# A two-block transformer with routed experts: routing split in two, a layer's norms placed between the combines, the output stored by token tiles

## The chip, the cores and the metric

The kernel runs on one core of a Trainium2 chip. All five engines of the core run their own instruction streams and meet only at semaphores: TensorE (PE, matmuls), VectorE (DVE), ScalarE (ACT), GpSimd (POOL) and SyncE (SP), which here only issues the loads of weights, the fetch of expert rows and the like. The metric is the device time of one execution in microseconds, lower is better.

## The reference

Everything is float32. Two blocks of two layers each run one after the other, on 256 tokens of width 1024. The first block (two attention mixers, each with a squared-ReLU MLP) is not touched by the change. The second block has an image stream `x` (256 tokens) and a context stream `ctx` (256 tokens); each of its two layers is a mixer and a mixture of experts. Layer 0 routes both streams (512 tokens), layer 1, the last, only `x` (256 tokens). Cut to what matters here:

```
def _moe(h, grp_w, grp_b, exp_w, exp_b, w_gate, w_up, w_down):
    g_logits = h @ grp_w + grp_b                      # 4 groups
    g_sel = argmax(g_logits);  g_w = softmax(g_logits)[g_sel]
    e_logits = (h @ exp_w + exp_b)[group g_sel]       # 8 experts of that group
    e_p, e_i = top_k(softmax(e_logits), 2)
    wts = g_w * e_p / sum(e_p)
    # each token goes to two of the 32 experts; each expert computes
    #   (silu(x @ w_gate[e]) * (x @ w_up[e])) @ w_down[e]
    # and a token's result is the weighted sum of its two rows
for i in range(2):
    hx, hc = modulate(rmsnorm(x)), modulate(rmsnorm(ctx))
    yx, yc = mixer(hx, hc);  x = x + g1 * yx          # ctx too in layer 0
    x = x + g2 * _moe(modulate(rmsnorm(x)), ...)      # ctx too in layer 0
```

An expert has 6 MB of weights, and each layer streams those of all 32 experts.

## The kernel before, in words

**Weights.** A ring of six slots of 2 MB holds weight tiles. SP issues one load for each tile, in one fixed order over the whole kernel (L1629 in its helper `load`), and waits before each until the tile that had the slot has been used. In a mixture-of-experts stage (`moe_loads`) an expert takes three tiles: gate, up, down. SP runs ahead of PE until the ring is full, so up to six tiles are there when the first expert begins.

**Routing.** `pe_moe` computes the logits of T token tiles of 128 (T is 4 in layer 0, 2 in layer 1; L985), and turns the tokens back to rows (L993), which ACT copies and stores to `tokens_d` (L1115, L1118). `dve_moe` then walks through one chain of small VectorE instructions, in which `do(...)` makes each wait for the one before: the best group of each token (L1204 to L1208), the two best experts in it (L1212 to L1218), one-hot marks `hot` of both picks (L1221), their sum `picked` (L1223) and its prefix over token tiles `prefix` (L1225). PE multiplies these by a strictly lower triangle and by ones (L999, L1000), which gives every token its rank within its expert. An expert's block has 64 slots; tokens beyond go to up to 15 overflow blocks. So DVE finds which experts have extra blocks and a running sum over experts (L1234 to L1244), each pick's position, block number and slot (L1248 to L1263), and makes two one-hot matrices, `slot_hot` and `blk_hot` (32 blocks and 15 overflow blocks, 47 columns; L1264 to L1270). PE multiplies them into a table of token ids for each block and slot (L1006). From it DVE computes `idx`, the rows to gather (L1282 to L1287), and `row`, where results go (L1291).

**Experts.** POOL gathers the 64 tokens of a block by an indirect DMA (L1363), two blocks ahead; PE turns them (L1017); DVE copies them out (L1309); PE runs gate and up (`inner`: L1026, L1029), turns the hidden rows (L1035) and runs down (`outer`: L1044), one expert behind; ACT applies silu (L1133) and copies the results out (L1136); POOL scatters them to `rows_d` (L1369). The hardware loop covers experts 1 to 30, with the last one and the overflow block behind it. Each engine reads the number of overflow blocks from memory into a register (`value_load`): before the experts on PE, ACT, DVE and POOL, behind the loads on SP (L1708 ff). With these inputs layer 0 has one overflow block and layer 1 has none.

**Combine.** When all rows are stored, SP fetches them by token tile (L1412); ACT weights the first row of each pair (L1178), and DVE adds the second, applies the gate and adds to the residual, three instructions for each tile (L1340, L1342, L1343), in layer 0 in the order ctx 0, ctx 1, x 0, x 1.

**The next layer's norms.** DVE makes the rotary tables (`rope_tables`, L2010, L2015) from three small loads that POOL issues once the rows are stored (L2152, L2154). `act_norm` squares and sums each token tile and takes the root (L350, L344), DVE divides (L365, L367), PE turns (L338), ACT and DVE evict four parts each (L387, L391). The ctx norm `L1.nc` runs whole and then the x norm `L1.nx`; then PE starts the projection (L438).

**End.** POOL stores both output tiles in one DMA of 1 MB (L2187) after the last combine.

## Time and profile before

| | |
|---|---|
| median of three runs | 2433.67 us (2433.35 to 2438.34) |
| the profiled execution, its own time | 2432.66 us |
| its span in the profile | 2430.8 us |
| PE / DVE / ACT / POOL busy, share of the span | 86% / 32% / 15% / 8% |
| granted TensorE clock, mean | 0.935 |
| layer 0's experts | about 1184 to 1715 us |
| layer 1's experts | about 1912 to 2402 us |
| weights of 65 expert blocks | 195 loads of 2048 KB |

Times in the profile are microseconds from the start of the span. 1.9 us of the execution's own time lie outside the span. The shares are means over stages with different limits: the page's row of forty slices shows the DMA engines at 9 tenths all through both expert stages, and close to idle just ahead of each. A clock of 1.00 is 2.4 GHz and 0.50 is 1.2 GHz.

### The profile page before, as it was taken

To read this page: it belongs to the slowest core of one execution; us is meant where nothing else is said; L and a number is where in the kernel's file an instruction comes from. 1 tells how busy PE (TensorE), PEld (TensorE's weight loads), DVE (VectorE), ACT (ScalarE), POOL (GpSimd) and SP (SyncE) were. 2 spreads that over 40 slices of the span, in tenths; PEclk is the share of its full clock that TensorE was granted. 3 is DMA by queue.
4 is the path that set the end of the run, shared out by engine and by line. 5 is a ranking of instruction groups with operands and counts; after the bars stand their busy time and mean duration, and the time that the engine had idled before them with its cause. 6 is when DMAs were issued, how large, how long until landed. Compare 5 with 4: busy or idle time off the path is not lost. (4 is left out here: it accounts for less than half of the span.)

```text
span 2430.8 us, 22184 instructions
## 1 busy us (share of the span) xinstructions
PE 2089.8 (86%) x8645; PEld 1111.1 (46%) x8645; DVE 768.4 (32%) x1684; ACT 360.5 (15%) x775; POOL 185.0 (8%) x225
## 2 busy tenths in 40 slices
PE   6998999998999998877698888888387798888884
PEld 3456666444666576435344343333254343333331
DVE  1225773214777118932311111101442310111111
ACT  2232000123100122421100000000232100000000
POOL 0000000000000000000011011111000011111110
PEclk9999999999999999998799899899799799999997
DMA  9931788341687503002499999999732499999994
GB/s 255 300 134 70 285 299 302 124 157 67 231 292 287 206 19 139 1 18 90 153 407 407 404 412 405 401 413 380 269 128 90 162 416 422 417 414 419 403 416 176
DMA packets 128053, 631.53 MB, mean 260 GB/s; under 512 B 14262, under 2 KB 16470, under 8 KB 102128
## 3 DMA queue, kind: packets, MB, share of 16 engines
q1 hardware_dynamic: 109056, 592.94, 62.0%
q0 software_dynamic: 17744, 34.33, 5.2%
q10 hardware_dynamic: 1184, 3.35, 0.4%
q8 instruction: 42, 0.69, 0.1%
q14 instruction: 27, 0.22, 0.0%
HBM read 625.47 MB, written 26.57 MB: 268 GB/s over the span
## 5 line engine op out<-in xcount | busy, mean ns | idle before, releaser
L1026 PE MATMUL PS<-ring,arena 128*64 128x512 f32 x1040 | 519.0, 657 | 112.5 <-DMA ring<-ex_up 110.6
L1029 PE MATMUL PS<-ring,arena 128*64 128x512 f32 x1040 | 519.8, 658 | 0.0
L1026 PEld LDWEIGHTS PS<-ring,arena 128*64 128x64 f32 x1040 | 151.1, 151 | 393.2 <-issue 382.6
L438 PE MATMUL PS<-ring,arena 128*128 128x512 f32 (+1 forms) x736 | 297.4, 560 | 7.6 <-issue 5.2
L1309 DVE COPY arena<-PS 128x512 f32<-128x512 f32 x64 | 44.3, 692 | 673.3 <-PE PS L1017 673.3
L1044 PE MATMUL PS<-ring,arena 128*64 128x512 f32 x1040 | 237.5, 598 | 1.6 <-DVE arena L1305 1.6
L757 PE MATMUL PS<-arena,ring 128*128 128x256 f32 x1024 | 226.6, 383 | 2.9 <-DVE arena L389 1.5
L768 PE MATMUL PS<-ring,arena 128*128 128x512 f32 x512 | 222.2, 592 | 0.0
L757 PEld LDWEIGHTS PS<-arena,ring 128*128 128x128 f32 x1024 | 194.8, 191 | 40.0 <-issue 13.7
L438 PEld LDWEIGHTS PS<-ring,arena 128*128 128x128 f32 x736 | 138.1, 191 | 147.5 <-issue 138.9
L1029 PEld LDWEIGHTS PS<-ring,arena 128*64 128x64 f32 x1040 | 151.0, 151 | 4.3
L768 PEld LDWEIGHTS PS<-ring,arena 128*128 128x128 f32 x512 | 97.2, 190 | 116.0 <-issue 115.3
L1133 ACT ACTIVATE arena<-PS 64x512 f32<-64x512 f32 x65 | 38.3, 590 | 663.3 <-PE PS L1026 652.1
L716 PE MATMUL PS<-ring,arena 128*128 128x512 f32 x288 | 126.7, 601 | 10.4 <-issue 9.6
L1044 PEld LDWEIGHTS PS<-ring,arena 128*64 128x64 f32 x1040 | 69.5, 136 | 118.1 <-issue 112.0
L1363 POOL DMA_INDIRECT arena<-tokens_d,arena x65 | 61.6, 947 | 697.0 <-PE PS L1017 619.6
L852 DVE SCALAR_TENSOR_TENSOR modacc<-ring,silu_c,modacc 128x512 f32<-128x512 f32 x168 | 112.8, 748 | 0.0
L852 DVE SCALAR_TENSOR_TENSOR xn<-ring,silu_c,xn 128x512 f32<-128x512 f32 x168 | 112.8, 747 | 0.0
L1017 PEld LDWEIGHTS PS<-const,arena 64*128 64x128 f32 x585 | 84.9, 245 | 60.8 <-issue 51.1
L338 PE MATMUL PS<-const,xn 128*128 128x128 f32 x176 | 35.6, 387 | 83.1 <-DVE xn L367 83.1
L1017 PE MATMUL PS<-const,arena 64*128 64x64 f32 x585 | 94.0, 304 | 9.4 <-DMA arena<-tokens_d,arena 9.4
L716 PEld LDWEIGHTS PS<-ring,arena 128*128 128x128 f32 x288 | 55.2, 193 | 80.3 <-issue 79.0
(229 smaller groups left out, 1653.6 us busy)
## 6 DMA issues: line engine op xcount, KB each, us to landing
ring<-ex_gate SPq DMA_DIRECT2D x65, 2048.0 KB, 16.8
ring<-ex_up SPq DMA_DIRECT2D x65, 2048.0 KB, 14.7
ring<-ex_down SPq DMA_DIRECT2D x65, 2048.0 KB, 24.0
ring<-ffn_w SPq DMA_DIRECT2D x32, 2048.0 KB, 12.8
ring<-mod_w SPq DMA_DIRECT2D x24, 2048.0 KB, 8.1
ring<-a_w_qkv SPq DMA_DIRECT2D x9, 2048.0 KB, 35.7
ring<-b_w_qkv SPq DMA_DIRECT2D x6, 2048.0 KB, 12.9
ring<-w_in_ab SPq DMA_DIRECT2D x3, 2048.0 KB
```

Source lines behind the costliest of these rows:

```text
L438: mm = pe.matmul(PS[:, u % 4, 0:w.width], q.src[:, k, w.t * P:(w.t + 1) * P], w8(w.tile, w.width)[:, k, :], start=(k == 0), stop=(k == KD ...
L716: mm = pe.matmul(PS[:, u % 8, :], x.src(k)[:, w.t * P:(w.t + 1) * P], rhs, start=(i == 0), stop=(i == len(w.terms) - 1))
L757: mm = pe.matmul(PS[:, b, (c % 2) * 2 * P:(c % 2 + 1) * 2 * P], w8(tile)[:, k, c * P:(c + 1) * P], XL[:, k, :], start=(k == 0), stop=(k == ...
L768: mm = pe.matmul(PS[:, 4 + 2 * t + h, :], hiddenT[:, half, c, t * P:(t + 1) * P], w4(tile)[:, c, h * BANK:(h + 1) * BANK], start=first and ...
L852: ins = dve.scalar_tensor_tensor(acc, w, silu_c[:, k, v:v + 1], acc, ALU.mult, ALU.add)
L1017: mm = pe.matmul(PS[:, 4 + u, k * CAP:(k + 1) * CAP], Xg[0:CAP, u, :].rearrange("p (m k) -> p k m", k=KD)[:, k, :], ident[0:CAP, 0:CAP], s ...
L1026: g = pe.matmul(PS[0:CAP, u, :], xT[:, k, :], w8(gate)[:, k, :], start=(k == 0), stop=(k == KD - 1))
L1029: h = pe.matmul(PS[CAP:P, u, :], xT[:, k, :], w8(up)[:, k, :], start=(k == 0), stop=(k == KD - 1))
L1044: mm = pe.matmul(PS[h * CAP:(h + 1) * CAP, 2 + u, :], hidT[:, k, :], w4(tile)[:, k, h * BANK:(h + 1) * BANK], start=(k == 0), stop=(k == 3))
L1133: act.activation(swish[CAP:P, :], PS[0:CAP, u, :], ACT.Silu).then_inc(done, 1)
L1309: dve.tensor_copy(XgT[:, u, :], PS[:, 4 + u, :]).then_inc(s.xT, 1)
L1363: pool.indirect_dma_start(out=Xg[0:CAP, u, :], out_offset=None, in_=tokens_d, in_offset=bass.IndirectOffsetOnAxis(ap=m.idx[0:CAP, blk:blk ...
```

## The change

- **Constants.** Token codes become `PLACES - code` (PLACES is 2048), so that an empty slot, a zero, maps by one multiply-add to an index past the end; `first` and `full` are new.
- **Routing, first part.** The group is found by a reduction, a comparison, a product and a reduction over all tiles at once. `prefix` is gone; PE makes the ranks from `picked` by one triangle product and T products with ones. `slot_hot` is made directly from the rank, and a first table of token ids has only the 32 experts' first blocks. One instruction gives `idx`, one gives `row`, and POOL starts to gather.
- **Routing, second part.** `place_overflow` (running sum, block, slot, marks of the overflow blocks, the number of extra blocks) stands on DVE behind `tokens_out(0, 0)`; its table of ids is a second pair of products on PE behind the hardware loop, and there the engines now read the number of blocks. The weights of the two picks come after the first hidden rows.
- **Token stores** of tiles 2 and 3 use their own buffer.
- **Norms.** In layer 0's combine DVE makes the rotary tables ahead of the first tile (`first`); the ctx norm's rows are made after the third tile (`after`). The x norm gets its own PSUM banks, columns and a scratch area; ACT sums x 0 ahead of evicting the ctx norm, and PE doesn't wait between the two norms.
- **Output.** SP stores each token tile, 512 KB, as soon as it is combined.

```
@@ pe_moe
-            pe.matmul(PS[:, 5, 0:(T + 1) * NE], ones, m.prefix..., start=True, stop=False)
-            mm = pe.matmul(PS[:, 5, 0:T * NE], C("before"), m.picked..., start=False, stop=True)
+            pe.matmul(PS[:, 5, 0:(T + 1) * NE], C("before"), m.picked..., start=True, stop=False)
+            for t in range(T):
+                mm = pe.matmul(PS[:, 5, (t + 1) * NE:(T + 1) * NE]..., ones,
+                               m.picked[:, t:t + 1, :].to_broadcast([P, T - t, NE]), start=False, stop=(t == T - 1))
-            pe.wait_ge(s.placed, b0.placed + 2)
...
-            pe.wait_ge(s.routed, b0.routed + 2)
+            def slot_ids(marks, first, width):
+                for half in range(2):
+                    for n in range(2 * T):
+                        mm = pe.matmul(PS[half * CAP:(half + 1) * CAP, 7, first:first + width], m.slot_hot[:, n, :],
+                                       marks[:, n, :], start=(n == 0), stop=(n == 2 * T - 1))
+                    mm.then_inc(s.ids, 1)
+            pe.wait_ge(s.placed, b0.placed + 1)
+            slot_ids(m.hot_token.rearrange("p j t e -> p (j t) e"), 0, NE)
             at(pe, (s.token_copied, T))
-            extra = pe.value_load(...)
...                                          # behind the loop over the experts
                 hidden_turned(e + 1)
+            pe.wait_ge(s.placed, b0.placed + 2)
+            slot_ids(m.over_hot, NE, OVER)
+            pe.wait_ge(s.routed, b0.routed + 2)
+            extra = pe.value_load(...)
             inner(NE - 1, 1, W.tail[0:2])
@@ dve_moe
-            do(dve.tensor_copy(m.g8[:, :, 0:EG], m.logits[:, :, 0:EG]))
-            for t in range(T):
-                do(dve.max(m.gtop[:, t, :], m.g8[:, t, :]))
-                do(dve.max_index(m.gidx[:, t, :], m.gtop[:, t, :], m.g8[:, t, :]))
-            do(dve.tensor_copy(m.gsel, m.gidx[:, :, 0]))
+            do(dve.tensor_reduce(m.gtop, groups, AX, ALU.max))
+            do(dve.tensor_tensor(m.gmark, groups, over(m.gtop, shape, 2), ALU.is_equal))
+            do(dve.tensor_tensor(m.gmark, m.gmark, over(C("first"), shape, 1), ALU.mult))
+            do(dve.tensor_reduce(m.gsel, m.gmark, AX, ALU.max))
...
-            do(dve.tensor_tensor(m.picked, m.hot[:, 0], m.hot[:, 1], ALU.add))
-            for t in range(T):
-                ins = dve.tensor_tensor(m.prefix[:, t + 1, :], m.prefix[:, t, :], m.picked[:, t, :], ALU.add)
+            dve.tensor_tensor(m.picked[:, 0:T, :], m.hot[:, 0], m.hot[:, 1], ALU.add).then_inc(s.picked, 1)
...
+            for j in range(2):
+                do(dve.tensor_tensor(m.hot_token[:, j], m.hot[:, j], over(code[j], shape, 2), ALU.mult))
             dve.wait_ge(s.rank, b0.rank + 1)
+            for j in range(2):
+                do(dve.tensor_tensor(m.tmp[:, j], m.hot[:, j], rank, ALU.mult))
+            do(dve.tensor_reduce(pos, tmp, AX, ALU.add))
+            dve.tensor_tensor(m.slot_hot, over(C("slot"), [P, n, CAP], 1), over(pos, [P, n, CAP], 2),
+                              ALU.is_equal).then_inc(s.placed, 1)
...
+            def rows_of(first, last, idx_done, row_done):
+                dve.wait_ge(s.ids, b0.ids + 1 + 2 * (first > 0))
+                idx_done(dve.tensor_scalar(m.idx[0:CAP, first:last], PS[0:CAP, 7, first:last], -0.25, PLACES / 4,
+                                           ALU.mult, ALU.add))
+                dve.wait_ge(s.ids, b0.ids + 2 + 2 * (first > 0))
+                row_done(dve.tensor_scalar(m.row[:, first:last], PS[:, 7, first:last], -2.0, C("half"),
+                                           ALU.mult, ALU.add))
...
             tokens_out(0, 0)
+            place_overflow()
             tokens_out(1, 1)
             hidden_out(0, 0, m.T.head[1])
+            weights()
...                                          # behind the loop
+            rows_of(NE, NB, ...)
+            dve.wait_ge(s.routed, b0.routed + 2)
+            extra = dve.value_load(...)
             hidden_out(NE - 1, 1, m.T.tail[1])
...
+            if first:
+                first()
             dve.wait_ge(second[m.l].s.gate2, ...)
             for n, t in enumerate(combine_order(T)):
...
+                if after:
+                    after(n)
@@ pool_moe
-            pool.wait_ge(s.routed, b0.routed + 2)
-            extra = pool.value_load(...)
+            pool.wait_ge(s.routed, b0.routed + 1)
...
                 if e == NE:
+                    pool.wait_ge(s.routed, b0.routed + 3)
+                    extra = pool.value_load(...)
@@ the streams of ACT, DVE, SP and POOL
-            act_norm(act, L1.nc)
-            at(act, L1.nc.turned)
-            act_norm(act, L1.nx)
+            act_norm_sums(act, L1.nc)
+            act.wait_ge(moes[0].s.combined, moes[0].b.combined + 3)
+            act_norm_sum(act, L1.nx, 0)
+            norm_out(act, L1.nc, 0)
+            act_norm_sums(act, L1.nx, tiles=(1,))
+            norm_out(act, L1.nx, 0)
...
-            dve_moe(dve, moes[0])
-            rope_tables(L1)
-            dve_norm(dve, L1.nc)
-            dve_norm(dve, L1.nx)
+            def norms_beside(n):
+                if n == 2:
+                    dve_norm_rows(dve, L1.nc)
+            dve_moe(dve, moes[0], first=lambda: rope_tables(L1), after=norms_beside)
+            at(dve, L1.nc.turned)
+            dve_norm_rows(dve, L1.nx)
+            norm_out(dve, L1.nc, 1)
+            norm_out(dve, L1.nx, 1)
...
+            for n, t in enumerate(combine_order(2)):
+                sp.wait_ge(moes[1].s.combined, moes[1].b.combined + n + 1)
+                sp.dma_start(out[0][t * P:(t + 1) * P, :], hx[:, t, :]).then_inc(s_out, 16)
...
-            pool.dma_start(out[0].rearrange("(t p) d -> p t d", p=P), hx[:, :, :]).then_inc(s_out, 16)
```

## Rows read from the trace of the kernel before

**Rows 1.** Windows: PE, PEld, DVE, ACT, POOL busy; clock; DMA share; GB/s.
```profile
1300.00:1680.00 380.00, 327.88 (x1450) 147.85 (x1448) 42.09 (x70) 27.63 (x47) 44.75 (x46) 0.92 1.01 408
1184.00:1194.00 10.00, 9.86 (x34) 3.04 (x35) 0.09 (x1) 0.20 (x1) 0.93 (x1) 0.74 0.03 7
```

**Rows 2.** Timeline of SP: start, duration, engine, line, what it issued.
```profile
1123.10 0.33 SPq L1629 DMA_DIRECT2D ring<-ex_gate  x1
1193.80 0.33 SPq L1629 DMA_DIRECT2D ring<-ex_up  x1
```

**Rows 3.** Timeline of layer 0's routing; in brackets the idle time before and its releaser.
```profile
1155.55 0.31 DVE L1202 TENSOR_TENSOR arena<-PS,arena 128x144 f32<-128x144 f32 x1 [12.36 <-issue]
...
1158.29 0.28 DVE L1212 TENSOR_TENSOR arena<-const,arena 128x128 f32<-128x128 f32 x1
...
1159.92 1.09 PE L993 MATMUL PS<-const,arena 128*128 128x128 f32 x8 [0.23 <-ACT xn L1115]
...
1162.32 0.87 DVE L1225 TENSOR_TENSOR arena<-arena 128x32 f32<-128x32 f32 x4
...
1163.24 0.54 PE L999 MATMUL PS<-arena,ones 128*128 128x160 f32 x2 [2.23 <-DVE arena L1225]
...
1164.04 0.29 DVE L1231 COPY arena<-PS 128x128 f32<-128x128 f32 x1 [0.85 <-PE PS L1000]
...
1174.34 3.25 PE L1006 MATMUL PS<-arena 128*64 128x47 f32 x32 [10.34 <-DVE arena L1270]
...
1176.78 0.18 DVE L1287 TENSOR_SCALAR arena<-arena 64x47 uint32<-64x47 f32 x1
...
1178.72 1.01 POOL L1363 DMA_INDIRECT arena<-tokens_d,arena  x1 [48.31 <-issue]
```

**Rows 4.** Group by line and shape on DVE: busy us, mean ns of one.
```profile
L1264 DVE TENSOR_TENSOR arena<-const,arena 128x512 f32<-128x512 f32 x1 | 0.7, 691 | 0.0
```

**Rows 5.** Timeline of layer 1's routing, half the token tiles.
```profile
1895.17 0.46 PE L999 MATMUL PS<-arena,ones 128*128 128x96 f32 x2 [2.01 <-DVE arena L1225]
...
1906.95 0.99 POOL L1363 DMA_INDIRECT arena<-tokens_d,arena  x1 [28.51 <-issue]
```

**Rows 6.** Timeline of layer 0's combine and of the norms behind it.
```profile
1719.42 0.56 POOL L2154 DMA_DIRECT2D arena<-k_norm_c  x1
...
1724.16 1.28 DVE L1340 SCALAR_TENSOR_TENSOR arena<-arena 128x1024 f32<-128x1024 f32 x1 [14.49 <-ACT arena L1178]
...
1734.02 1.04 ACT L350 ACTIVATE xn<-arena 128x1024 f32<-128x1024 f32 x1
...
1737.84 0.29 ACT L344 ACTIVATE small<-small,const 128x1 f32<-128x1 f32 x1
...
1740.47 0.28 DVE L2010 TENSOR_TENSOR arena<-arena 128x128 f32<-128x128 f32 x1
...
1741.41 0.16 DVE L365 RECIPROCAL small<-small 128x1 f32<-128x1 f32 x1
...
1754.74 14.00 PE L438 MATMUL PS<-ring,arena 128*128 128x512 f32 x32 [1.77 <-DVE arena L391]
```

**Rows 7.** DMA issues: KB each, median us from issue to landing.
```profile
arena<-k_norm_c POOLq DMA_DIRECT2D x1, 32.0 KB, 8.8
```

**Rows 8.** Timeline at the end of the experts: SP's loads, PE's waits.
```profile
1671.61 0.33 SPq L1629 DMA_DIRECT2D ring<-ex_down  x1
1673.61 0.35 SPq L1712 DMA_DIRECT2D ring<-ex_gate  x1
...
1697.95 1.12 PE L1026 MATMUL PS<-ring,arena 128*64 128x512 f32 x1 [3.11 <-DMA ring<-ex_up]
...
2385.51 0.61 PE L1026 MATMUL PS<-ring,arena 128*64 128x512 f32 x1 [0.47 <-DMA ring<-ex_up]
```

**Rows 9.** DMA issues: KB each, median us from issue to landing.
```profile
out<-hx POOLq DMA_DIRECT2D x1, 1024.0 KB, 4.5
...
tokens_d<-xn ACTq DMA_DIRECT2D x4, 512.0 KB, 2.7
```

More of the change, by code:

```diff
@@ L87, in shape_constants @@
     parts["slot"] = np.tile(np.arange(CAP), (P, 1))
-    parts["block"] = np.tile(np.arange(NB), (P, 1))
+    parts["block"] = np.tile(np.arange(OVER), (P, 1))
     parts["expert"] = np.tile(np.arange(NE), (P, 1))
-    parts["group"] = np.tile(np.arange(NE) // EPG, (P, 1))
+    parts["group"] = np.tile(EG - np.arange(NE) // EPG, (P, 1))
+    parts["first"] = np.tile(EG - np.arange(EG), (P, 1))
+    parts["full"] = np.tile(CAP * np.arange(1, FULL + 1), (P, 1))
     parts["over"] = np.tile(np.repeat(np.arange(OVER), NE), (P, 1))
     token = p[:, None, None] + P * np.arange(4)[None, None, :]
-    parts["token"] = 4 * token + np.arange(2)[None, :, None] + 1
-    parts["half"] = p[:, None] // CAP
+    parts["token"] = PLACES - (4 * token + np.arange(2)[None, :, None])
+    parts["half"] = 2 * PLACES + p[:, None] // CAP
     parts["eps"] = np.full((P, 1), EPS)
@@ L1179, in act_moe, with dve_moe @@
                    .then_inc(s.weighted, 1)
-        def dve_moe(dve, m):
+        def dve_moe(dve, m, first=None, after=None):
             s, b0, T, n = m.s, m.b, m.tiles, 2 * m.tiles
@@ L1243, in dve_moe @@
-            through = x
-            do(dve.tensor_tensor(m.before, through, m.extra, ALU.subtract))
-            tmp = m.tmp.rearrange("p j t e -> p (j t) e")
-            for j in range(2):
-                do(dve.tensor_tensor(m.tmp[:, j], m.hot[:, j], m.rank, ALU.mult))
-            do(dve.tensor_reduce(flat(m.pos), tmp, AX, ALU.add))
-            do(dve.tensor_tensor(tmp, hot, over(m.before, [P, n, NE], 1), ALU.mult))
-            do(dve.tensor_reduce(flat(m.start), tmp, AX, ALU.add))
-            pos, start, turn, spill = flat(m.pos), flat(m.start), flat(m.turn_no), flat(m.spill)
@@ L1262, in dve_moe @@
-            do(dve.tensor_tensor(blk, blk, esel, ALU.add))
-            do(dve.scalar_tensor_tensor(slot, turn, -float(CAP), pos, ALU.mult, ALU.add))
-            dve.tensor_tensor(m.slot_hot, over(C("slot"), [P, n, CAP], 1), over(slot, [P, n, CAP], 2),
-                              ALU.is_equal).then_inc(s.placed, 1)
-            do(dve.tensor_tensor(m.blk_hot, over(C("block"), [P, n, NB], 1), over(blk, [P, n, NB], 2),
-                                 ALU.is_equal))
-            for j in range(2):
-                part = m.blk_hot[:, j * T:(j + 1) * T, :]
-                ins = dve.tensor_tensor(part, part, over(C("token")[:, 4 * j:4 * j + T], [P, T, NB], 2), ALU.mult)
-                if j:
-                    ins.then_inc(s.placed, 1)
@@ L1298, in dve_moe @@
-            dve.sem_inc(s.weights_ready, 1)
-            extra = dve.value_load(m.regs[0:1, OVER:OVER + 1], min_val=0, max_val=m.over)
+            dve.tensor_tensor(m.picked[:, 0:T, :], m.hot[:, 0], m.hot[:, 1], ALU.add).then_inc(s.picked, 1)
+            dve.tensor_scalar(m.ngtop, m.gtop, -1.0, None, ALU.mult).then_inc(s.group_top, 1)
+            dve.tensor_tensor(m.gap, m.etop[:, :, 1], m.etop[:, :, 0], ALU.subtract).then_inc(s.expert_gap, 1)
+            code = [C("token")[:, 4 * j:4 * j + T] for j in range(2)]
@@ L1592, in moe_stage @@
             m.pos, m.start, m.turn_no = take(2, tiles), take(2, tiles), take(2, tiles)
-            m.spill, m.blk, m.slot = take(2, tiles), take(2, tiles), take(2, tiles)
-            m.slot_hot, m.blk_hot = take(n, CAP), take(n, NB)
+            m.blk, m.slot = take(2, tiles), take(2, tiles)
+            m.slot_hot, m.over_hot = take(n, CAP), take(n, OVER)
             m.idx, m.row = take(NB, dt=U32), take(NB, dt=U32)
-            m.empty, m.code = take(NB), take(NB)
             m.full_before = take(OVER, NE)
```

180 lines of the change are left out of this document (92 added, 88 removed).

## The prediction

> **What bounds the kernel now.** I read the page's forty slices first: the DMA engines are at 9 tenths through both expert stages and nearly idle in the slices ahead of each. The windows say the same with a number: over 380 us of layer 0's experts the DMA share is 1.01 and 408 GB/s flow [rows 1]. PE is the busiest engine by share, but there it waits for tiles. So the expert stages last as long as their weights take to stream, and what can be gained is the time in which the stream stands. SP's timeline shows that time. A load is issued at 1123.10 and the next at 1193.80 [rows 2]: the ring is full, and its first slot comes free only when PE has done gate and up of expert 0. That needs the gather, which needs the routing. Layer 1 repeats the pattern. Every microsecond by which a first gather comes earlier starts the stream earlier, and as the amount of data is the same, it ends earlier by as much. The same holds for the norms between the layers, where PE waits from the end of the experts until 1754.74 [rows 6], and for the last store, which nothing follows.
>
> The chain of layer 0's routing is in the timeline [rows 3]: logits at 1155.55, first ranks product at 1163.24, ranks read at 1164.04, ids product at 1174.34, idx done at 1176.78 + 0.18 = 1176.96, gather at 1178.72. All but PE's share is small DVE instructions: one of 0.18 us costs 0.21 with its gap to the next.
>
> **Routing, layer 0.** From the end of the logits' step (1155.89) to L1212 (1158.29) 2.40 us are spent on the group. Four small steps replace it, 0.82: 1.6 saved. One cast in place of two and the gap moved away: 0.3. The prefix, 0.87, goes. `picked` would be ready at 1162.32 - 1.9 = 1160.45. But PE is still turning the last token tile until 1159.92 + 1.09 = 1161.0, and the ranks wait behind it. The new ranks product is five float32 products, ten pieces, where there were two in four pieces, 1163.24 to 1164.04, 0.20 each. Narrower pieces gain nothing visible, so I price by the piece: 1.9 to 2.0 us. Ranks are there at 1163.0, 1.0 us earlier than before. (Bounds: priced by columns, 480 against 288, it is 1.35; by pieces 2.0.) The two multiplies by the code lie under it.
>
> Then come two multiplies at 0.33 (as the copy of ranks, 0.29, with its gap), a reduction of 256 columns between those and the 0.69 of 512 columns [rows 4], say 0.45, and `slot_hot`, 0.69 plus the signal: 1.85. PE starts the ids at 1164.9, not 1174.34. From there to idx took 2.62 before, with three DVE steps; one remains, so 2.2. The count of full blocks (three steps, 1.0 us) lies under PE's half of the ids. idx is done at 1167.1, 9.9 us earlier. POOL then no longer loads a register ahead of the gather. SP's timeline prices that: from 1671.94 to 1673.61 it does two loads and a branch [rows 8], so about 0.8 for one. Layer 0 gains 10.7. (Bounds: 9.4 with a free-standing rank penalty of 0.5 more and no gain at POOL, 11.5 with ranks by columns and no wait left but 0.8.) The token stores land 2.7 us after issue [rows 9], before that time.
>
> **Routing, layer 1.** Half the tiles. The group's part shrinks from 2.40 to about 1.43 and the new one is again 0.82: 0.6. Casts 0.3, prefix 0.43. The ranks start at 1895.17 - 1.35 = 1893.8 [rows 5], PE being free; three products, 1.2. The four DVE steps at half width, between 0.18 and layer 0's values, 1.35; eight pieces of ids (3.25 / 32 = 0.10 each) with latency 0.9; idx 0.2; POOL 0.8. The gather starts at 1898.25, not 1906.95 [rows 5]: 8.7. (Bounds 7.5 to 9.5.)
>
> **The second part** stands behind `tokens_out(0, 0)`. DVE's queue behind it is `tokens_out(1, 1)` and the hidden rows of expert 0, and PE waits for those only after gate and up of expert 0, which fill the window 1184 to 1194 [rows 1]. Twelve scan steps, about fifteen small ones, a `slot_hot` at 0.69 and two row-0 steps near 0.6 make 7.2 us against 9.5 of cover. Cost nothing; without cover it would be up to 7.2.
>
> **Behind the loop** PE gets 32 pieces of ids in layer 0 (3.25) and 16 in layer 1 (1.6), and a register load, 0.75. In layer 0 the overflow block absorbs part: PE waited 3.11 us there for its weights [rows 8], 2.4 of it usable after ACT's copy, and a little before expert 31. 4.0 - 2.8 leaves 1.2. In layer 1 PE runs from 2385.51 through to the end of the experts with only 0.47 of waiting ahead [rows 8], so 2.35 - 0.5 = 1.9 is on the path. POOL's scatter of expert 28 now waits for the second ids; expert 30's copy, a gate and up and a down product later, is the first to need it. Bounds: 0 and 6.3 together. I take 3.1.
>
> A rule of the Trainium skill bears on the register load: "Runtime: NRT & Kernel Launch", section "Instruction fetch mechanics", gives about 0.2 us for a bulk register load from HBM. By that the two insertions would cost 1.1 less and the two gathers gain 1.1 less; the sum would stay.
>
> **Norms.** Before, four combines follow each other, then tables, then the ctx norm, then the x norm. The new order hides the ctx norm beside the last combine, and PE needn't wait between norms. But `first` puts the tables ahead of the combines, and they need three POOL loads. The last is issued at 1719.42 and takes 8.8 us to land [rows 6, 7]: 1728.2. The tables take 0.94 (1740.47 to 1741.41), so the first combine starts at 1729.2, not 1724.16. Behind it on DVE is everything. Combines of 3.75 us (three of up to 1.28) end at 1732.95, 1736.7 and 1740.4. ACT's sums of ctx take from 1734.02 to 1738.13 before, 4.1; they now start at 1736.75 and end at 1740.85. DVE makes the ctx rows until 1742.4 and the last combine until 1746.2. ACT's sum for x 1 ends 1.5 later, 1747.8; its row is ready at 1748.8; DVE then evicts four parts of ctx and four of x, 1.95 each, until 1752.7. PE starts at 1752.75 where it was 1754.74 [rows 6]: 2.0 gained. With the tables free it would be 5.5. The weights of this projection are there by then either way.
>
> **Store.** The last tile's 512 KB go from SP. The token stores of that size landed in 2.7 us, the whole output took 4.5 [rows 9]: 1.8. The first tile's store lies under the second combine. What follows the landing I take as unchanged.
>
> Against splitting speaks the Trainium skill, "DMA: Bandwidth & Descriptors", section "Anatomy of one DMA": about 2 us fixed per DMA plus bytes over 436 GB/s. It gives 4.4 for the whole, as the trace does, and 3.2 for a half, so 1.2 gained, and 0.6 less in the sum.
>
> **Sum.** -10.7 - 8.7 + 3.1 - 2.0 - 1.8 = -20.1. The profiled execution took 2432.66 (span 2430.8 and 1.9 around it), 1.0 below the median. 2433.67 - 20.1 = 2413.5.
>
> **Rivals.**
> - *The tables don't hold the combines* (the loads land by 1724): 3.5 more, 2410.0. For it: nothing but that the loads are small. Against: the row of 8.8.
> - *The clock stays up.* In 1184 to 1194 it was 0.74 on average [rows 1], that is about 5.2 us at 1.2 GHz and the rest at 2.4. PE now stands idle less before expert 0. If the whole product ran at 2.4 GHz it would end 2.6 earlier, in both layers: 2408.3. Against: the pieces between are few and narrow, and the gather's wait remains.
> - *Insertions behind the loop uncovered* and ranks dearer: 3.2 more, 2416.7.
> - *Slower: the stream loses rate.* It moves the same bytes at 408 GB/s [rows 1] for some 980 us in both layers. If the gathers and the first loads fell so that it ran at 395, that would be 32 us, and 2445. It decides from a loss of 2.1%; below 1.6% the kernel is faster. Nothing in the loop changes, which speaks against it.
>
> **Chances.** Forecast 0.58, tables free 0.10, clock up 0.12, insertions dearer 0.10, stream slower 0.10, of which 0.06 ends above +0.2% and 0.04 near nothing. A measurement of this kernel can tell 0.2%, about 5 us, from no change. Faster 0.90, same 0.04, slower 0.06. The range reaches from tables free and clock up together (2405) to the dear insertions with the routing at its lower bounds and 2 us for the run (2421).
>
> **What would show it.** First gathers at 10.7 and 8.7 us less after the logits; ten pieces of ranks in about 2 us; the first combine held by L2154's loads near 1729 in old time; ids behind the loops with PE going straight on; the last store landing 2.7 us after issue. Wrong would be: a stall of DVE behind `tokens_out(0, 0)` that reaches PE, another rate of the stream, or the copy of expert 30 waiting for a late scatter.

## The result and the profile after

The changed kernel took 2397.03 us (median of 4 executions, 2396.06 to 2405.25) where the kernel before took 2435.93 on the same chip (4, 2433.35 to 2438.34): ratio 0.9848, 95% interval 0.9822 to 0.9874. The forecast was 2413.5, range 2405 to 2421. The direction was right. The gain was nearly twice the one foretold, and the time lies under the range. Of three later series of the changed kernel one gave the same gain, and two, both on one other chip, smaller ones (28.9 us), so the size needs care; the experiments come back to it.

The profiled execution took 2405.25, the longest of the four, span 2403.4. I go through it in the prediction's order, with the lines that answer to those of before.

**Routing, layer 0** (timeline: start, duration, engine, line, operation; in brackets the idle time ahead and its releaser), to be held against [rows 3]:

```profile
1159.58 0.31 DVE L1218 TENSOR_TENSOR arena<-PS,arena 128x144 f32<-128x144 f32 x1 [11.83 <-issue]
...
1165.01 0.44 PE L1008 MATMUL PS<-arena,const 128*128 128x160 f32 x2
...
1165.29 0.97 PE L1011 MATMUL PS<-arena,ones 128*128 128x128 f32 x8
...
1166.37 0.61 DVE L1246 TENSOR_TENSOR arena<-arena,PS 128x128 f32<-128x128 f32 x2 [1.21 <-PE PS L1011]
...
1168.21 1.85 PE L1019 MATMUL PS<-arena 128*64 128x32 f32 x32 [1.95 <-DVE arena L1249]
...
1169.44 0.18 DVE L1261 TENSOR_SCALAR arena<-PS 64x32 uint32<-64x32 f32 x1 [0.34 <-PE PS L1019]
...
1170.63 1.01 POOL L1386 DMA_INDIRECT arena<-tokens_d,arena  x1 [35.32 <-DVE arena L1261]
```

From the logits to the first gather 11.05 us pass, in place of 23.17 (1155.55 to 1178.72): 12.1 gained, forecast 10.7. The ten pieces of ranks took 1.25 from first to last (1165.01 to 1166.26), not 2.0. The ids' first half took about half of 1.85, and idx followed at 1169.44, 1.23 behind the start of the ids; I had allowed 2.2 up to the end of idx, which came at 1169.62, 1.41. POOL started 1.01 behind idx, where it had been 1.76 (1176.96 to 1178.72): the step without the register load is 0.75 shorter, where the load was priced at about 0.8. No run takes the load out alone.

The clock had a part in this that the forecast didn't price. Windows (PE, PEld, DVE, ACT, POOL busy; granted clock; DMA share; GB/s), first of before, then of after, around the ids product:

```profile
1174.00:1178.00 4.00, 3.25 (x32) 3.09 (x32) 2.80 (x12) 0.20 (x1) 0.00 (x0) 0.50 0.00 0
```

```profile
1168.00:1170.20 2.20, 1.85 (x32) 1.73 (x32) 1.32 (x6) 2.17 (x11) 0.00 (x0) 1.00 0.45 182
```

Before, PE had stood idle 10.34 us ahead of the ids and made them at 0.50; now it stands 1.95 and makes them at 1.00. Layer 1 separates the clock from the width. Timelines of PE, of the kernel before, the changed kernel, and p2, a run described below with the same routing:

```profile
1903.16 1.54 PE L1006 MATMUL PS<-arena 128*64 128x47 f32 x16 [7.34 <-DVE arena L1270]
```

```profile
1885.89 0.91 PE L1019 MATMUL PS<-arena 128*64 128x32 f32 x16 [1.42 <-DVE arena L1249]
```

```profile
1885.57 1.51 PE L1019 MATMUL PS<-arena 128*64 128x32 f32 x16 [1.42 <-DVE arena L1249]
```

The granted clock was 0.50, 1.00 and 0.50 in these three stretches. 16 pieces of 47 and of 32 columns cost the same at 0.50, 1.54 and 1.51, and 0.91 at 1.00: the clock sets the price here, not the width.

**Routing, layer 1**, against [rows 5] (timelines; before, then after):

```profile
1890.35 0.23 DVE L1202 TENSOR_TENSOR arena<-PS,arena 128x72 f32<-128x72 f32 x1 [6.00 <-issue]
```

```profile
1879.82 0.23 DVE L1218 TENSOR_TENSOR arena<-PS,arena 128x72 f32<-128x72 f32 x1 [5.02 <-issue]
...
1887.77 0.99 POOL L1386 DMA_INDIRECT arena<-tokens_d,arena  x1 [18.87 <-DMA tokens_d<-xn]
```

From its logits to its first gather 7.95 us pass, in place of 16.60 (1890.35 to 1906.95): 8.65 gained, forecast 8.7. The gather's releaser is new: the last store of tokens, issued at 1884.27, lands at 1886.92, 0.09 after idx is done (1886.65 + 0.18). A still shorter index would gain nothing in this layer as long as that store stays where it is.

**SP's timeline**, against [rows 2]: the load that waits for expert 0's slot went out at 1185.41, not 1193.80. All of the logits' 4.03 us of delay is in that figure: they came at 1159.58, not 1155.55, before any changed instruction.

```profile
1127.96 0.33 SPq L1656 DMA_DIRECT2D ring<-ex_gate  x1
1185.41 0.33 SPq L1656 DMA_DIRECT2D ring<-ex_up  x1
```

**Loop ends**, against [rows 8] (timeline of PE):

```profile
1669.37 1.83 PE L1019 MATMUL PS<-arena 128*64 128x15 f32 x32
...
1689.91 1.11 PE L1040 MATMUL PS<-ring,arena 128*64 128x512 f32 x1 [1.82 <-DMA ring<-ex_up]
...
2365.02 0.90 PE L1019 MATMUL PS<-arena 128*64 128x15 f32 x16
```

The ids stand behind the loops, and cost 1.83 and 0.90 where I had priced 3.25 and 1.6. The price came from pieces made at a clock of 0.50; these ran at 1.00 (windows 1669.00 to 1671.50 and 2364.50 to 2366.50), and 32 columns at 1.00 took 1.85 and 0.91, so again it is the clock and not the 15 columns. PE still waits 1.82 for the overflow block's weights, where it waited 3.11.

**Norms**, against [rows 6] (timeline of DVE, then PE):

```profile
1719.73 0.29 DVE L2043 TENSOR_TENSOR arena<-arena 128x128 f32<-128x128 f32 x1 [17.94 <-DMA arena<-k_norm_c]
...
1720.68 1.28 DVE L1362 SCALAR_TENSOR_TENSOR arena<-arena 128x1024 f32<-128x1024 f32 x1
...
1743.52 15.70 PE L447 MATMUL PS<-ring,arena 128*128 128x512 f32 x32 [2.52 <-DVE arena L400]
```

DVE stood 17.94 us for `k_norm_c`, built the tables and began to combine at 1720.68: the wait that the forecast named. PE's projection starts at 1743.52, 11.2 us earlier than before, 2.9 of them beyond the 8.37 by which layer 0 as a whole ended earlier (SP fetched its rows at 1717.75 and now at 1709.38). But the first 32 pieces now take 15.70, not 14.00: the granted clock was 0.66 in their first 5 us, where it was 1.00 before. Layer 1's next ring load keeps only 1.2 of the 2.9.

**The end** (timeline of SP and DVE, then the page's DMA issues), against [rows 9]:

```profile
core 0 of [0], span 2403.4 us
...
2396.70 4.05 SPq L1760 DMA_DIRECT2D out<-hx  x2
...
2399.16 1.22 DVE L1365 TENSOR_TENSOR hx<-hx,arena 128x1024 f32<-128x1024 f32 x1
```

```profile
out<-hx SPq DMA_DIRECT2D x2, 512.0 KB, 2.6
```

The last sum ends at 2400.38 and the span at 2403.4, 3.0 later. Before (timeline of DVE, then of POOL):

```profile
core 0 of [0], span 2430.8 us
...
2417.50 1.22 DVE L1343 TENSOR_TENSOR hx<-hx,arena 128x1024 f32<-128x1024 f32 x1
...
2419.03 0.78 POOL L2187 DMA_DIRECT2D out<-hx  x1 [15.51 <-DVE hx L1343]
```

The last sum ended at 2418.72, the store landed near 2423.5 (2419.03 + 4.5), and the span ended at 2430.8: 12.1 behind the sum, of which 7.3 lie behind the landing. Behind SP's landing (about 2403.0) lie 0.4. **The tail (from the last sum to the end of the span) shrank by 9.0 us where I had 1.8.**

### The profile page after: what moved, and what is told of

It reads as the page before. It is cut to its first block and busy times, and to the rows that moved or that the text cites. A ratio compares the mean times of both kernels' runs of the same rounds, so it can differ in the third digit from the quotient of the medians.

```text
span 2403.4 us, 22261 instructions
## 1 busy us (share of the span) xinstructions
PE 2094.6 (87%) x8701; PEld 1103.5 (46%) x8701; DVE 763.2 (32%) x1644; ACT 361.4 (15%) x775; POOL 185.5 (8%) x224
## 6 DMA issues: line engine op xcount, KB each, us to landing
ring<-a_w_qkv SPq DMA_DIRECT2D x9, 2048.0 KB, 48.3
```

## The experiments

Theory A: the stages add up, and the miss lies mainly in the tail, because a store from POOL's queue holds the end of the program long after it has landed. Theory B: the tail is small and the gain is something that the profiled pair doesn't show. The rivals of single edits are in their expectations.

All traces were cut at the same marks: logits on DVE, first gather, the load that restarts the ring, SP's fetch of layer 0's rows, `ex_up` of layer 1's first ring, layer 1's first gather, ring and fetch, the end of the last sum, the span's end. This table is worked out from their timelines. The column `logits` is the time in the span, each other column the us from the mark before it to its own:

```
                     logits gather  ring fetch0 ex_up gather1 ring1 fetch1   sum   end
before              1155.55  23.17 15.08 523.95 51.03 138.17 14.34 483.60 13.85 12.06
s3 before, SP tiles 1159.30  23.57 13.90 522.17 51.30 137.84 14.68 486.42 14.13  3.09
s4 before, SP whole 1153.36  23.15 15.05 521.30 53.01 138.59 14.51 483.75 13.90  4.48
r0 routing only     1154.98  10.77 14.15 525.01 54.06 130.43 14.07 486.65 14.09 11.99
n1 norms undone     1155.39  10.77 14.07 522.57 51.28 128.94 14.10 486.19 13.94  3.05
changed             1159.58  11.05 14.78 523.97 49.86 128.53 14.67 484.03 13.91  3.02
s1 changed          1160.81  11.24 14.94 525.83 50.82 130.38 14.05 486.22 14.01  3.00
a2 changed          1161.08  11.22 14.90 525.88 50.77 130.39 14.00 486.14 14.03  3.09
a3 changed          1155.24  11.01 14.39 520.06 50.02 128.56 14.55 483.51 13.96  3.00
s2 POOL store       1153.02  10.93 14.27 519.91 50.27 129.94 13.81 486.09 13.74 12.02
p2 small POOL load  1162.16  10.92 13.91 522.50 48.20 130.18 14.89 487.35 13.82 11.27
n2 early tables     1160.02  11.02 14.61 519.86 46.23 130.40 13.99 486.78 13.82  3.07
n3 early tables     1157.89  10.76 14.17 525.09 45.04 130.01 13.70 486.15 14.07  3.02
w2 23 fillers       1159.88  11.02 14.59 522.19 45.18 130.03 15.40 486.83 14.05  3.03
w1 46 fillers       1159.74  11.02 14.60 519.58 61.45 128.93 14.13 486.22 13.79  3.04
r1 overflow first   1163.35  10.89 17.09 525.17 48.48 130.04 16.09 484.79 13.94  3.06
r2 delay            1163.55  19.48 14.70 522.88 48.34 137.77 14.71 484.15 13.98  3.04
```

The stages that no edit touches vary by themselves: up to the logits 1153 to 1164, layer 0's stream (fetch0) 519.6 to 525.9, layer 1's 483.5 to 487.4, in kernels of every kind. One profile against another can thus be off by 10 us, while routing, norms and end repeat to a fraction of that.

### The tail

**s1, the changed kernel again, nothing edited.**

> The changed kernel once more, unaltered, for its median and for a second profile. Theory A (the terms read from the two profiles are the whole change: routing 12.1 and 9.3, norms 1.2, tail 9.0, nothing else): about 31 us less than the kernel before, ratio 0.987. Theory B (a gain that the profile of the changed kernel hides, because it stood 4 us later already at layer 0's logits): about 37 us less, ratio 0.985, and logits near 1155 or earlier in the new profile.

2398.25 us (2393.78 to 2413.14, 5 executions), ratio 0.9847 [0.9825, 0.9870]. The size came again on this chip, and the end at 3.00 us too. The ratio is Theory B's (0.985), though its interval reaches 0.987; the logits came at 1160.81, not by 1155 as Theory B wanted.

**s2, the changed kernel with POOL's one store as before.**

```
-  (SP) for n, t in enumerate(combine_order(2)): ... sp.dma_start(out[0][t * P:(t + 1) * P, :], hx[:, t, :])
+  (POOL) at(pool, *moes[1].done)
+  (POOL) pool.dma_start(out[0].rearrange("(t p) d -> p t d", p=P), hx[:, :, :]).then_inc(s_out, 16)
```

> The changed kernel with the output stored as before: one DMA of 1 MB, issued by POOL after the last combine. Theory A (the end of the kernel waits some 7 us longer behind a store from POOL than behind one from SP): 9 us slower than the changed kernel, with 7 us between landing and the end of the span. Rival (only the landing of a smaller store was gained, 1.8 us, as predicted): 2 us slower.

2416.38 (2405.77 to 2419.90), ratio 0.9923 [0.9906, 0.9941]. DVE's last line and POOL's:

```profile
core 0 of [0], span 2404.0 us
...
2390.74 1.22 DVE L1365 TENSOR_TENSOR hx<-hx,arena 128x1024 f32<-128x1024 f32 x1
...
2392.26 0.78 POOL L2219 DMA_DIRECT2D out<-hx  x1 [15.38 <-DVE hx L1365]
```

From 2391.96 to 2404.0: 12.0 again, 9.0 more than the changed kernel. Its median lies 18 us over that of s1 on the same chip, twice what its trace shows; against all 21 timed executions of the changed kernel (median 2404.4, below) it is 12.

**s3 and s4, the kernel before with its output from SP: in two tiles, and whole.**

```
-  (POOL) pool.dma_start(out[0].rearrange(...), hx[:, :, :])
+  s3 (SP) for n, t in enumerate(combine_order(2)): ... sp.dma_start(out[0][t * P:(t + 1) * P, :], hx[:, t, :])
+  s4 (SP) at(sp, *moes[1].done); sp.dma_start(out[0].rearrange("(t p) d -> p t d", p=P), hx[:, :, :])
```

> The kernel before with only the store changed: two DMAs of 512 KB from SP, each after its combine. Theory A: 9 us faster than before, ratio 0.9963. Rival (landing only): 1.8 us faster, ratio 0.9993.

> The kernel before with its one store of 1 MB issued by SP, not split. If the engine that issues makes the difference: about 7 us faster than before, ratio 0.997, landing still 4.5 us after issue and under 1 us from landing to the end. If splitting makes it: no difference from before.

2428.21, ratio 0.9964 [0.9947, 0.9980], and 2426.00, ratio 0.9964 [0.9951, 0.9976]: 8.8 us each, whether split or not. The last rows of s4's timeline, and its DMA issue:

```profile
core 0 of [0], span 2421.1 us
...
2415.39 1.23 DVE L1343 TENSOR_TENSOR hx<-hx,arena 128x1024 f32<-128x1024 f32 x1
...
2416.64 0.39 SPq L1732 DMA_DIRECT2D out<-hx  x1
```

```profile
out<-hx SPq DMA_DIRECT2D x1, 1024.0 KB, 4.0
```

End 4.5 us behind the sum for the whole, 3.1 for the tiles, 12.1 from POOL. Splitting is worth 1.4 and the issuing engine 7.6. Of the 7.6, 0.5 is a shorter landing (4.0 in place of 4.5). My 1.8 for the splitting was a little high. The Trainium skill, "DMA: Bandwidth & Descriptors", section "Anatomy of one DMA", made it 1.2. Its fit is stated for transfers issued from GpSimd, and these go from SP; the rows (4.0 against 2.6) give 1.4, nearer to the page than to my 1.8.

**p2, the changed kernel with one small load more from POOL behind the last sum.**

```
+  at(pool, *moes[1].done)
+  pool.dma_start(sinks[:, 0, :], ins["sink_c_2"][0:1, :].to_broadcast([P, 8])).then_inc(s_band.sinks, 16)
+  pool.wait_ge(s_band.sinks, 32)
```

> The changed kernel, its output stored by SP in two tiles, with one more transfer from POOL behind the last combine: the 8 sink values again, broadcast to 128 partitions (4 KB), with a wait for it. Theory A (what stands behind POOL's store is a fixed cost of POOL's queue at the end, whatever it carries): the span ends 9 us or so after the transfer's issue or later, that is 10 to 12 us behind the last combine in place of 3.0. Rival (the 7.3 us go with the 1 MB that the store writes): it ends 3 to 5 us behind the last combine, by the small transfer's own landing of some 2 to 3 us.

One execution, 2417.02 us; its rows:

```profile
core 0 of [0], span 2415.2 us
...
2402.70 1.22 DVE L1365 TENSOR_TENSOR hx<-hx,arena 128x1024 f32<-128x1024 f32 x1
...
2404.22 0.59 POOL L2223 DMA_DIRECT2D small<-sink_c  x1 [15.49 <-DVE hx L1365]
```

The output goes from SP as in the changed kernel, and yet the span ends 11.3 us behind the sum: 11.0 from the issue of 4 KB, against 11.8 from the issue of 1 MB before. So the cost hardly depends on what POOL moves. The page gives 5.3 for the landing as the median of this kernel's two loads of that kind, and the first took 7.0 in the changed kernel, so the last one landed about 3.6 after its issue: 7.4 lie behind it, as 7.3 lay behind the 1 MB. That falls in Theory A's favour. In the changed kernel POOL's last transfer, a scatter, was issued at 2384.14, 19 us ahead of the end; 11 us after it are over by 2395, so its end can't show such a cost. Each run with the late end has both a last transfer from POOL and POOL's wait for it, and no run parts the two.

### The norms

**n1, the changed kernel with the norms' part undone** (tables and both norms behind the four combines; the x norm in the ctx norm's banks and scratch).

```
-  dve_moe(dve, moes[0], first=lambda: rope_tables(L1), after=norms_beside)
...
+  dve_moe(dve, moes[0])
+  rope_tables(L1)
+  dve_norm(dve, L1.nc)
+  dve_norm(dve, L1.nx)
```

> The changed kernel with the norms behind the combines and the rope tables behind them again, as in the kernel before. Theory A (the norms' part is worth 2.9 us at the projection's first piece, of which 1.2 us reach the stream): fetch to first piece 37 us in place of 34.1, the ring's ex_up for layer 1 some 1.2 to 2.9 us later against the fetch, time 2400 and ratio 0.9855. Rival (the norms carry the 9 us by which the prediction missed): ratio 0.989.

2408.43, ratio 0.9903 [0.9882, 0.9924], on a chip where the changed kernel wasn't timed. That is the rival's 0.989 and not Theory A's 0.9855. By the trace, though, fetch to the projection's first piece takes 37.25, and fetch to `ex_up` 51.28. Over the traces: 49.6 on average in the eight with the changed norms (changed, s1, a2, a3, s2, p2, r1, r2), 52.1 in the five without (before, s3, s4, r0, n1). **The norms are worth 2.5 us at the ring**, by means over stages that spread over 2.6 and 3.0 us. The start of the projection is sharper: 33.9 to 34.5 behind the fetch in the eight, 37.0 to 37.3 in the five, 2.9 us earlier. What blurs it at the ring is the clock at the projection's start. Where the first 32 pieces took 14.0 (p2, r1 and r2, against before, s3 and n1), `ex_up` comes after 48.3 and 51.2; where they took 15.7 to 17.0 (changed, s1, a2, a3 and s2, against s4 and r0), after 50.4 and 53.5: 2.9 and 3.2 at like clocks. The timing would allow more (some 11 us against the mean of the changed kernel's four ratios, on other chips); no stage of its trace shows it. On its own chip n1 took 7.2 us more than n2 below, where the stages give 2.5 + 4.0 = 6.5.

**n2 and n3, the rope tables' loads issued early** (the same kernel in two series).

```
-  pool_moe(pool, moes[0])
   rope_loads(L1, "q_norm_c_2", "k_norm_c_2")
+  pool_moe(pool, moes[0])
```

> The changed kernel with POOL's loads for the rope tables (k_norm_c among them) issued ahead of layer 0's routing and gathers instead of behind the last gather. Theory A (what holds the first combine is the tables' wait for k_norm_c, 17.9 us of idle VectorE of which the combines inherit 5): the tables are built while VectorE idles in the expert loop, the first combine starts with its rows and not behind the tables, and from the fetch of layer 0 to the projection's first piece pass some 29 us in place of the changed kernel's 34.1 (1709.4 to 1743.5); the start of layer 1's ring moves by 3 to 5 us, the time from 2398 to about 2394, ratio about 0.983. Rival: the transfer that the combines wait for is the rows' own fetch and the clock of TensorE at the projection's start takes back the rest: under 1 us, ratio unchanged at 0.985.

> The kernel with early tables again, for the comparison on one chip with the changed kernel and with the one that keeps TensorE busy. By the traces so far it is 3 to 4.6 us ahead of the changed kernel from layer 0's fetch to layer 1's ring (46.2 us against 48.2 to 50.8): ratio against the changed kernel 0.998 to 0.9985. Rival (its first timing, ratio 0.9873 against 0.9847 and 0.9865, was no chance): 1.001 or above.

2401.23, ratio 0.9873 [0.9851, 0.9895], and 2399.01, ratio 0.9842 [0.9817, 0.9868] beside 2404.65 and 0.9873 [0.9848, 0.9899] for the changed kernel on that chip (a3). The trace (DVE, PE) shows the mechanism:

```profile
1697.97 0.29 DVE L2043 TENSOR_TENSOR arena<-arena 128x128 f32<-128x128 f32 x1
...
1711.98 1.29 DVE L1362 SCALAR_TENSOR_TENSOR arena<-arena 128x1024 f32<-128x1024 f32 x1 [12.98 <-ACT arena L1195]
...
1734.81 16.90 PE L447 MATMUL PS<-ring,arena 128*128 128x512 f32 x32 [1.65 <-DVE arena L400]
```

The tables are made under the last expert, the combine waits for its rows on ACT and for nothing else, and the fetch (1705.51) is 29.3 us from the projection, not 34.1. Fetch to `ex_up` is 45.6 on average: 4.0 less than in the changed kernels; at the projection's start it is 4.9 (29.2 and 29.3 against 34.2). So the named wait is real, and the prediction's 3.5 for its removal was somewhat low. The two intervals of n3 and a3 overlap; by the timings alone the gain of 5.6 us isn't secured, by the stage it is. The first series' ratio is no better than the changed kernel's elsewhere.

**w1 and w2, TensorE kept busy in its idle stretch**, on top of the early tables. Nothing reads the bank. w1 has 46 products ahead of the norms and 3 between them, w2 23 and 2.

```
+  def warm(n):
+      for _ in range(n):
+          pe.matmul(PS[:, 6, :], ident, const[:, 0:BANK], start=True, stop=True)
+  warm(23)
   pe_norm(pe, L1.nc)
+  warm(2)
   pe_norm(pe, L1.nx)
```

> The kernel with the tables' loads issued early, and on TensorE 46 products of 512 columns from the constant table into a bank that is free, between layer 0's last down projection and layer 1's first norm, and 3 more between the two norms; nothing reads them. Theory A (the granted clock of 0.5 at the projection's start, 16.9 us for 32 pieces in place of 14.0, comes from TensorE's idle time of some 22 us ahead of the norms): clock 1.0 from 1700 on, first 32 pieces 14.0 us, fetch to ex_up 43 us in place of 46.2, and the time about 2396 on a chip where the early tables gave 2399. Rival (the clock falls for another reason, or the fillers themselves run at the low clock and hold up the norms' transposes): no gain, or up to 10 us later.

> As the last kernel with products on TensorE in its idle stretch, but 23 of them (19.9 us by the 0.432 us that each of the two passes of one took) in place of 46, and 2 between the norms. Theory A (the projection starts at the low clock because TensorE idles ahead of it): the fillers end near 1722, 2 us ahead of the norm's first transposes; projection's first 32 pieces 14.0 us in place of 16.9, fetch to ex_up 43 to 44 us in place of 46.2, and 2 to 3 us less than the kernel with early tables. Rival: the clock falls in the norms' own gaps all the same, and nothing is won.

w1: 2414.69, ratio 0.9903 [0.9876, 0.9930], 7 us over the changed kernel on that chip (a2). Its own timeline says why: the 46 products are 92 records, 39.7 us at full clock, twice what I had reckoned, and the norm's transposes stand behind them.

```profile
1701.97 39.74 PE L1868 MATMUL PS<-const 128*128 128x512 f32 x92 [0.90 <-ACT arena L1151]
...
1741.55 1.91 PE L344 MATMUL PS<-const,xn 128*128 128x128 f32 x16
```

w2: 2394.64, ratio 0.9841 [0.9816, 0.9866], against n3's 0.9842, and fetch to `ex_up` 45.2 against 45.0: nothing won. (The medians, on one chip, are 4.4 apart; both kernels' executions spread over 10 us and more.) Windows (PE, PEld, DVE, ACT, POOL busy; granted clock; DMA share; GB/s), first of n2, then of w2:

```profile
1710.00:1715.00 5.00, 0.00 (x0) 0.00 (x0) 2.95 (x3) 2.30 (x2) 0.00 (x0) 0.50 1.01 426
...
1735.00:1740.00 5.00, 5.00 (x6) 1.97 (x7) 0.00 (x0) 0.00 (x0) 0.00 (x0) 0.50 1.03 380
```

```profile
1710.00:1715.00 5.00, 5.00 (x13) 2.23 (x12) 0.76 (x1) 1.15 (x1) 0.00 (x0) 1.00 0.98 406
...
1725.00:1730.00 5.00, 3.61 (x20) 2.38 (x20) 4.86 (x8) 4.15 (x10) 0.00 (x0) 1.00 1.08 366
1730.00:1735.00 5.00, 2.71 (x17) 2.13 (x16) 4.34 (x9) 2.52 (x6) 2.85 (x4) 0.88 1.05 387
1735.00:1740.00 5.00, 3.06 (x5) 1.39 (x5) 2.01 (x5) 0.86 (x2) 0.00 (x0) 0.50 1.07 391
```

The fillers do hold the clock at 1.00, that is 2.4 GHz, from 1710 on. But the norms' own stretch leaves PE idle for 1.4 us of 5 and then for 2.3, and it is back at 0.50, 1.2 GHz, when the projection starts at 1737.07; the first 32 pieces took 15.76, as in n3 (15.78). The rival was right: the fillers lift the clock through the long wait, and it falls again in the norms' gaps. Those gaps alone don't decide it: six traces without fillers (before, s3, n1, p2, r1, r2) have such gaps too and started the projection at 1.00. What decides stays open.

### The routing

**r0, the kernel before with the routing's part alone** (norms as in n1, POOL's store as in s2).

> The kernel before with the routing's part of the change alone (norms behind the combines and rope tables behind them, POOL's one store of 1 MB). Theory A (the parts add up: routing 12.1 less 0.2 in layer 0 and 9.3 less 0.4 in layer 1, norms and tail as before): from logits to first gather 11.05 us, 12 us behind the last combine, some 21 us under the kernel before, ratio 0.9915. Rival (the routing is also what made the executions' clock better, and holds the several microseconds by which the medians differ more than the stages): 28 us, ratio 0.9885.

2417.63 (2408.62 to 2424.78), ratio 0.9914 [0.9886, 0.9941]: 21 us under before. The two routing parts, 12.2 and 8.7, sum to 20.9; the interval reaches from 14 to 28, so that the agreement to the microsecond is luck.

**r1, the overflow placed ahead of the first tokens' way out.**

```
-  tokens_out(0, 0)
   place_overflow()
+  tokens_out(0, 0)
```

> The changed kernel with the overflow placed before layer 0's first tokens go out on VectorE, in place of beside the first expert. Theory A (where it stands, its 7.2 us lie under the first expert's gate and up; put ahead, VectorE's part of it delays the first expert's input): the stream's restart against the first gather, 14.8 us in the changed kernel, becomes 17 to 22 us. Rival (VectorE has that time to spare while the gathers and the transposes run): the same 14.8 us.

Gather to ring takes 17.09 in layer 0, where the thirteen other traces with the new routing lie between 13.9 and 14.9 (mean 14.5), and 16.09 in layer 1 (others 13.7 to 15.4, mean 14.3): 2.6 and 1.8 us lost. One execution, but both layers show it. The 7.2 us of the second part aren't free anywhere; where the change puts them, between DVE's copy of the first tokens and PE's end of gate and up, no cost is seen (14.5 against 14.7 in the three traces with the old routing).

**r2, a delay on the way to the first gather**, 13 products of 480 elements ahead of idx in both layers.

```
+  spin = m.full_before.rearrange("p b e -> p (b e)")
+  for _ in range(13):
+      do(dve.tensor_tensor(spin, C("over"), C("over"), ALU.mult))
```

> The changed kernel with 13 products of 480 elements added on VectorE ahead of the slot indices in both layers, some 8.7 us each. Theory A (every microsecond of routing on the way to the first gather is passed on to the end): from logits to first gather 19.8 us in place of 11.05 in layer 0, the stream's restart later by the same 8.7 us, the same again in layer 1, and about 17.4 us at the last combine against the logits. Rival (part of the routing's gain is absorbed by the queue or the ring): the end moves by less than 12 us.

One execution, 2424.52 us, 20 over the changed kernel's median of 2404.4. Logits to gather 19.48, 8.4 more; layer 1's gather 137.77, 8.3 more than the changed kernels' 129.5. The stages behind them lie inside their usual scatter (14.70, 522.88, 48.34, 14.71, 484.15). From the first logits to the last sum it took 1256.0, 13.1 more than the mean of the changed kernel's four traces, where 16.7 were put in and the rival asked for less than 12; the single traces lie 8.5 to 20 below it. So no stage is seen to absorb the delay, and most of it, at the least, reaches the end; that all of it does is inside the scatter and not shown to the microsecond.

**a2 and a3, the changed kernel in two more series.**

> The changed kernel a third time, on the chip of the two others, to compare them with it. If the difference to the stages' sum of 27 to 31 us is variation from one execution and chip to the next: a ratio between 0.984 and 0.988, with one of its ends nearer to 0.988. If it belongs to the change: 0.985 again.

> The changed kernel, on the chip of these two. By the stages 27 to 31 us under the kernel before, ratio 0.9875 to 0.989; by the first two timings 0.985, by the third 0.9865.

2407.85, ratio 0.9865 [0.9841, 0.9890], and 2404.65, ratio 0.9873: 28.9 us both. With the first two series there are 21 executions of the changed kernel, median 2404.4, and 48 of the kernel before beside them, median 2436.3: **31.9 us**. The stages give the same. Routing 12.2 and 8.7 (mean of the four traces of the changed kernel against the three with the old routing), norms 2.5, end 9.0: 32.4. The means of the same executions differ by 33.7. So the first ratio's 39 us lies high and the profiled pair's 27.4 low, and for Theory B a microsecond or so is left. 31.9 lies inside all four intervals. Chance of execution is enough to explain the spread; as both small gains come from one chip and s1's large one from another, a difference between chips isn't ruled out.

## Why the prediction missed, step by step

- **The step that failed** is the last clause of the store: "What follows the landing I take as unchanged." 7.3 us lay behind the landing of POOL's store, 0.4 lie behind SP's. s2, s3, s4 and p2 show the late end with POOL's transfer and the early one with SP's, in both kernels and with 4 KB. The rows were at hand: store issued 2419.03, landing 4.5, span 2430.8. I read the landing and didn't subtract it from the span. The store's term was 1.8 and measured 9.0. Of the miss against 31.9, 11.8 us, it makes 7.2; the terms below make the rest. With it alone the forecast would have been 2406.3, inside its range, and the changed kernel's 21 executions have their median at 2404.4; the further 7 us down to 2397.03 lie within the spread between series, and no stage shows a cause for them.
- **Routing, layer 0**: mechanism right, gain 12.2 by the means in place of 10.7. The ranks went by columns (1.25 us, at a clock of 1.00 both before and after), near my lower bound of 1.35. The ids' first half was priced at the 0.50 of before and ran at 1.00, which gives the other 0.7. The measured 12.2 lies beyond my bound of 11.5, for that reason. **Layer 1**: 8.7 forecast; 8.8 measured from its own logits to its first gather (16.6 in the three traces with the old routing, 7.8 on average in the four of the changed kernel), and 8.7 by the table's stage.
- **The second part** under gate and up at no cost: no cost is seen, and r1 shows the price of another place.
- **Behind the loop**: 3.1 looks too dear. The profiled pair gives 0.0 in layer 0 (523.95 and 523.97) and 0.4 in layer 1, and the means of these stages differ by 1.5 and 0.4, together 1.9, with a spread of 6 and 4 us. So it lies somewhere between 0 and 2, and no run isolates it. Two premises of the price were wrong. The pieces were priced at a clock of 0.50 and ran at 1.00: 1.83 and 0.90, not 3.25 and 1.6. And the waits that were to cover them were read from one trace: 3.11 and 0.47 there, but 1.4 and 2.0 in s3 and s4, where the same code stands. That a late scatter held a copy in layer 0 is seen (ACT's copy at 1683.26 is released by it), but PE waits for the overflow block's weights until 1689.91 in any case.
- **Norms**: the wait for `k_norm_c` came as foretold, and PE's start gained 2.9 in place of 2.0. 2.5 reach the ring by the means, 2.9 to 3.2 between traces with a like clock at the projection's start; that clock was low in five of the eight traces with the new norms and in two of the five with the old.
- **Stream**: 408 GB/s in the same window as before, so the slower rival is out.

```profile
1300.00:1680.00 380.00, 325.24 (x1474) 140.40 (x1472) 42.76 (x72) 27.64 (x47) 43.90 (x45) 0.92 1.01 408
```

- **Tables free**, given 0.10, did not come; n2 had to make it. **Clock up** did not come in the product that it named, gate and up of expert 0: the clock was 0.76 in its 10 us, against 0.74 in [rows 1], and gather to ring took 14.78 against 15.08, in the same scatter of 13.9 to 15.1 as before. It came in the ids product instead, where it was worth 0.7.

```profile
1176.00:1186.00 10.00, 10.00 (x36) 3.22 (x35) 6.18 (x26) 0.58 (x1) 0.71 (x1) 0.76 0.03 7
```

## What to carry to other kernels

Subtract the last transfer's landing from the end of the span: what remains is a term too, and here it was worth more than the splitting that the edit was about. Issue the last transfer from SP and not from POOL where SP is free. When a small product is priced from a trace, read the granted clock of its stretch too: here a shorter chain ahead of it also changed the clock. When something is put ahead of a chain, look at what it waits for: the loads of tables that depend on nothing belong ahead of the stage, not ahead of their use.

## What the runs showed of the hardware

- A program whose last transfer is POOL's ends 11.0 to 11.8 us after its issue, with 4 KB and with 1 MB alike; with SP's it is 4.5 for 1 MB. 7.3 to 7.4 of it lie behind the landing (1 MB and 4 KB), 0.4 to 0.5 with SP. What fills them isn't seen in any row and stays open.
- A float32 product of 512 columns by 128 rows stands in the trace as two records of 0.43 us at full clock, 0.86 together (x92 for 46 products, 39.74 us).
- Narrow pieces of the ids product cost by the piece and the clock: about 0.095 us each at 0.50 with 47 or 32 columns (16 in 1.54 and 1.51), 0.057 at 1.00 with 32 or 15 columns (16 in 0.91 and 0.90).
- The granted clock is 0.50 in PE's long idle stretch ahead of the norms (n2, 1710 to 1715); kept at 1.00 by work that nobody reads, it was at 0.50 again behind the norms' stretch, in which PE was idle for 1.4 us and then for 2.3 us of 5 (w2). Without fillers the projection started at 1.00 in six traces and lower in nine.
- Executions of one kernel on one chip range over up to 19 us (2393.78 to 2413.14), and a longer one comes with a lower mean granted clock (0.941 against 0.931). That is as large as most parts of this change, which is why stages cut at fixed marks told more than the medians.
